# Experts' gather from fp32 token rows, and what is loaded in the places that this frees

## The reference

```python
# block 1
x = x + merged @ w_out                      # after attention and convolution branches
h2 = rms_norm(x, norm_ffn_g)                # 256 tokens x 1024
# router: top-1 of 4 groups, then top-2 of the 8 experts in that group
for g in range(N_GROUPS):                   # 4 groups x 8 experts, D_EXPERT = 256
    act = silu(h @ w_gate[g]) * (h @ w_up[g])
    act = act * combine[:, g]
    y = y + act @ w_down[g]
x = x + y
# block 2: attention and gated MLP mixer, layer norm, a dense SwiGLU (hidden 2816), layer norm
```

## Time and profile before

| | |
|---|---|
| runs | 699.73, 701.96, 703.51 us (median 701.96) |
| profiled execution | span 705.1 us; no other time of this execution is given |
| PE busy | 651.5 us, 92% |
| DVE / ACT / POOL busy | 336.3 us, 48% / 254.8 us, 36% / 18.2 us, 3% |
| moved by DMA | 186.06 MB, mean 264 GB/s |
| chain that ended last | PE 83%, DMA 8%, DVE 4%, issue 2% |

### The profile page before, as it was taken

How to read it: one execution, slowest core, us unless ns; L and a number is a source line. 1 busy time by engine, 2 the same in 40 slices (tenths; PEclk the granted TensorE clock), 3 DMA queues, 4 the chain that set the end, 5 groups by cost and what they waited for, 6 DMA issues and landing times.

```text
span 705.1 us, 11554 instructions
## 1 busy us (share of the span) xinstructions
PE 651.5 (92%) x4977; PEld 537.3 (76%) x4977; DVE 336.3 (48%) x417; ACT 254.8 (36%) x317; POOL 18.2 (3%) x11
## 2 busy tenths in 40 slices
PE   6999999999989988658877999999999999999995
PEld 5889999998856655335533577778889999999994
DVE  6754448756461121001110466776847444444447
ACT  6555453643411111000100455774146333333330
POOL 0000000000100000000000001420000000000000
PEclk9999999999999999976999999997999999999998
DMA  8969434787999999999999999153535555750001
GB/s 322 407 181 402 160 127 165 248 305 261 407 373 406 399 402 410 421 418 419 420 412 408 389 408 370 61 185 115 173 129 183 193 194 193 250 178 0 0 1 59
DMA packets 96219, 186.06 MB, mean 264 GB/s; under 512 B 9648, under 2 KB 33328, under 8 KB 96176
## 3 DMA queue, kind: packets, MB, share of 16 engines
q1 hardware_dynamic: 95888, 185.36, 70.8%
q10 hardware_dynamic: 288, 0.07, 0.0%
HBM read 184.37 MB, written 1.05 MB: 263 GB/s over the span
## 4 chain that ended last, share of the span: by engine, by line
PE 83%; DMA 8%; DVE 4%; issue 2%; SPq 1%; ACT 1%; DVEq 0%; ACTq 0%
PE ps L681 20%; PE ps L682 20%; PE ps L683 20%; DMA ring<-in_w_down_e 5%; PE ps L929 3%; PE ps L1003 3%; PE ps L958 3%; PE ps L1024 2%; PE ps L973 2%; PE ps L1036 2%; DMA ring<-in_w_up_e 2%; DMA X<-in_x 1%; PE ps L740 1%; SPq L508 1%; PE ps L813 1%
## 5 line engine op out<-in xcount | busy, mean ns | idle before, releaser
L1390 ACT ACTIVATE w_hi<-ring 128x2048 fp32r<-128x2048 f32 (+1 forms) x77 | 139.6, 1837 | 6.1 <-DMA ring<-in_w_in 5.6
L1844 DVE TENSOR_TENSOR w_lo<-ring,w_hi 128x2048 fp32r<-128x2048 f32 x47 | 107.4, 2296 | 34.2 <-ACT w_hi L1390 34.0
L681 PE MATMUL ps<-xT_hi,w_hi 128*128 128x256 f32 x320 | 90.6, 283 | 0.0
L683 PE MATMUL ps<-xT_hi,w_lo 128*128 128x256 f32 x320 | 90.6, 283 | 0.0
L682 PE MATMUL ps<-xT_lo,w_hi 128*128 128x256 f32 x320 | 90.5, 283 | 0.0
L681 PE MATMUL ps<-hR_hi,w_hi 128*128 128x256 f32 x224 | 64.0, 286 | 0.0
L682 PE MATMUL ps<-hR_lo,w_hi 128*128 128x256 f32 x224 | 63.4, 283 | 0.0
L683 PE MATMUL ps<-hR_hi,w_lo 128*128 128x256 f32 x224 | 63.3, 283 | 0.0
L682 PEld LDWEIGHTS ps<-xT_lo,w_hi 128*128 128x128 f32 x320 | 61.4, 192 | 0.4
L681 PEld LDWEIGHTS ps<-xT_hi,w_hi 128*128 128x128 f32 x320 | 61.4, 192 | 0.3
L683 PEld LDWEIGHTS ps<-xT_hi,w_lo 128*128 128x128 f32 x320 | 61.4, 192 | 0.0
(11 more groups left out here) (327 smaller groups left out, 1214.8 us busy)
## 6 DMA issues: line engine op xcount, KB each, us to landing
ring<-in_w_in SPq DMA_DIRECT2D x28, 1024.0 KB, 13.4
ring<-in_w_up_e SPq DMA_DIRECT2D x28, 1024.0 KB, 13.7
ring<-in_w_gate_e SPq DMA_DIRECT2D x27, 1024.0 KB, 11.8
ring<-in_w_down_e SPq DMA_DIRECT2D x26, 1024.0 KB, 16.7
ring<-in_w_gate SPq DMA_DIRECT2D x11, 1024.0 KB, 5.5
ring<-in_w_up SPq DMA_DIRECT2D x11, 1024.0 KB, 5.5
ring<-in_w_down SPq DMA_DIRECT2D x11, 1024.0 KB, 4.8
ring<-in_w_out SPq DMA_DIRECT2D x8, 1024.0 KB, 9.9
```

What stands on the lines that cost most here:

```text
L681: mm(o, a_hi, b_hi, start=start, stop=False, skip_group_check=True)
L683: return mm(o, a_lo, b_hi, start=False, stop=stop, skip_group_check=True)
L1390: return nc.scalar.activation(o, i, ACT.Copy)
L1844: tt(w_lo[slot][:], ring[:, slot, :], f32(upper_of(i)), ALU.subtract).then_inc(lo_made, 1)
```

## The change

`gather` reads `X` in fp32 with `pick` seen as fp32, and `xs_hi` and `xs_lo` are gone with their semaphores. `X` stays where it is until the experts are done. `early_c` moves to 176 KiB (over `ga`), a twelfth early unit `early_e` is put in four pieces of 2 KiB per partition (162, 200, 202 and 220 KiB), and both are loaded when `mgT_made` is 2. Four units are loaded again instead of three. `junk2`, a place for results that nobody reads, moves.

```diff
-EARLY = 11
-AGAIN = 3
+EARLY = 12
+AGAIN = 4
...
-        early_c = at("early_c", 168, [P, UNIT])
+        early_c = at("early_c", 176, [P, UNIT])
+        early_e = [at("early_e%d" % j, kib, [P, UNIT // QUAD]) for j, kib in enumerate((200, 202, 162, 220))]
...
-        junk2 = at("junk2", 220, [P, D], BF16)
+        junk2 = at("junk2", 192, [P, D], BF16)
...
         EARLY_AT = [(early_a, 0), (6, B1_PROJ), (7, B1_PROJ), (4, B1_UNITS - 4), (5, B1_UNITS - 4),
-                    (0, B1_UNITS - 3), (1, B1_UNITS - 2), (2, B1_UNITS - 1), (3, B1_UNITS), (early_b, 0), (early_c, 0)]
+                    (early_c, 0), (early_e, 0), (0, B1_UNITS - 3), (1, B1_UNITS - 2), (2, B1_UNITS - 1), (3, B1_UNITS),
+                    (early_b, 0)]
...
                     src = (wge if u < 4 else wue)[q, :, :, 2 * (u % 4):2 * (u % 4) + 2, :]
+                    if isinstance(dst, list):
+                        for j, part in enumerate(dst):
+                            sp.dma_start(part.rearrange("p (k f) -> p k f", k=2), src[:, j]).then_inc(landed, 16)
+                        return
...
-                elif spot is early_c:
-                    sp.wait_ge(xacc_ps, 1)
-                    sp.wait_ge(xslo_made, 1 + 2)
+                elif spot is early_c or spot is early_e:
+                    sp.wait_ge(mgT_made, 2)
...
                 if m == GU:
-                    early_unit(GU + 3)
-                    early_unit(GU + 4)
+                    for n in range(GU + 3, GU + 7):
+                        early_unit(n)
...
-                    early_unit(GU + 5 + m - GU)
+                    early_unit(GU + 7 + m - GU)
...
-            def gather(features, s, waits=False):
-
-                for part in range(2):
-                    for t in range(T):
-                        for k in features:
...
-                            last = mm(ps[:, 6 + k // 4, (k % 4) * P:(k % 4 + 1) * P], xs_lo(t, k) if part else xs_hi[:, t, k, :],
-                                      pick[:, t, :], start=(part == 0 and t == 0 and k % 4 == 0),
-                                      stop=(part == 1 and t == T - 1), skip_group_check=True)
+            def gather(features, s):
+
+                for t in range(T):
+                    for k in features:
+                        last = mm(ps[:, 6 + k // 4, (k % 4) * P:(k % 4 + 1) * P], X[:, t, k:D:KD],
+                                  pick[:, t, :].bitcast(F32), start=(t == 0 and k % 4 == 0), stop=(t == T - 1),
+                                  skip_group_check=True)
...
-                copy(xs_hi[:, t], X[:, t, :].rearrange("p (q k) -> p k q", k=KD)).then_inc(xshi_made, 1)
...
-            for dst, ks in ((xs_lo1a, slice(0, KD // 2)), (xs_lo1b, slice(KD // 2, KD))):
-                x = X[:, 1, :].rearrange("p (q k) -> p k q", k=KD)
-                tt(dst[:], x[:, ks, :], f32(xs_hi[:, 1, ks, :]), ALU.subtract).then_inc(xslo_made, 1)
...
-            xs_lower(0, ((xs_lo0, slice(0, KD)),))
```

More of the change, by code:

```diff
@@ L296, in build @@
         zy_ready = sem("zy_ready")
-        xshi_made = sem("xshi_made")
-        xslo_made = sem("xslo_made")
         h2a_made = sem("h2a_made")
@@ L301, in build @@
         wr_made = sem("wr_made")
-        xacc_ps = sem("xacc_ps")
         land_early_d = sem("land_early_d")
@@ L433, in early_area @@
             spot = EARLY_AT[early_spot(n)[0]][0]
+            if spot is early_e:
+                return [part[:] for part in early_e]
             return early[:, spot, :] if isinstance(spot, int) else spot[:]
@@ L546, in _ @@
                              ).then_inc(land_early_d, 16)
-            for n in range(GU + EARLY - 2, GU + EARLY):
-                early_unit(n)
+            early_unit(GU + EARLY - 1)
             for n in range(RING + EARLY + 1, 4 * UPQ):
@@ L911, in _ @@
             mm(ps[:, 7, 2 * NE:3 * NE], ones_b, asg[:, 1, :], start=False, stop=True).then_inc(rank_ps, 1)
[L912 to L918, removed]
-            def gather(features, s, waits=False):
-                for part in range(2):
-                    for t in range(T):
-                        for k in features:
[L925 to L928, removed]
-                            last = mm(ps[:, 6 + k // 4, (k % 4) * P:(k % 4 + 1) * P], xs_lo(t, k) if part else xs_hi[:, t, k, :],
-                                      pick[:, t, :], start=(part == 0 and t == 0 and k % 4 == 0),
-                                      stop=(part == 1 and t == T - 1), skip_group_check=True)
-                            if part and t == T - 1 and k % 4 == 3:
-                                last.then_inc(s["gath_ps"], 1)
+            x_in(0, 0)
+            def gather(features, s):
[4 more added lines that the diff above has]
+                                  skip_group_check=True)
+                        if t == T - 1 and k % 4 == 3:
+                            last.then_inc(s["gath_ps"], 1)
             def slot_weights(it, s):
@@ L980, in keep_busy, with quad_hidden @@
                     mm(ps[:, bank, 0:3 * P], ident_b, bfc[:].rearrange("p a n -> p (a n)"), start=True, stop=True)
-            def quad_hidden(it, s, weights, landed, waits=False, wide=False, fill=0):
+            def quad_hidden(it, s, weights, landed, wide=False, fill=0):
                 pe.wait_ge(s["pick_made"], it * 2 + 1)
                 pe.wait_ge(s["y_made"], it * 2 + 1)
-                gather(range(0, 6), s, waits)
+                gather(range(0, 6), s)
                 pe.wait_ge(s["turned_made"], it * 2 + 1)
@@ L996, in quad_hidden @@
                     wv = weights(u)
-                    if len(wv.shape) == 2:
-                        wv = wv.rearrange("p (a x) -> p a x", a=2)
-                    wv = wv.rearrange("p a (j k f) -> p a j k f", j=2, k=2)
+                    if isinstance(wv, list):
+                        rows = [part.rearrange("p (k f) -> p k f", k=2) for part in wv]
+                    else:
+                        if len(wv.shape) == 2:
+                            wv = wv.rearrange("p (a x) -> p a x", a=2)
+                        wv = wv.rearrange("p a (j k f) -> p a j k f", j=2, k=2)
+                        rows = [wv[:, j // 2, j % 2] for j in range(QUAD)]
                     for kk in range(2):
@@ L1003, in quad_hidden @@
                             last = mm(ps[32 * j:32 * j + 32, 4 + u // 4, 0:FE], heT[:, k, 32 * j:32 * j + 32],
-                                      wv[:, j // 2, j % 2, kk, :], start=(k == 0), stop=(k == KD - 1))
+                                      rows[j][:, kk, :], start=(k == 0), stop=(k == KD - 1))
                     last.then_inc(s["used"], 1)
@@ L1038, in quad_spread, with quad @@
                 last.then_inc(s["spread"], 1)
-            def quad(it, s, weights, landed, waits=False, wide=False):
-                quad_hidden(it, s, weights, landed, waits, wide)
+            def quad(it, s, weights, landed, wide=False):
+                quad_hidden(it, s, weights, landed, wide)
                 if wide:
@@ L1066, in wait @@
                         k, value = early_spot(n)
-                        pe.wait_ge(land_early[k], value)
+                        pe.wait_ge(land_early[k], value * (QUAD if EARLY_AT[k][0] is early_e else 1))
                     else:
@@ L1085, in _ @@
             for q in range(WIDE):
-                quad(q, first, weights_of(q), landed_of(q), q == 0)
+                quad(q, first, weights_of(q), landed_of(q))
             with pe.Fori(WIDE, OVER) as q:
@@ L2170, in _ @@
             slots(0, start0, 1)
-            dve.wait_ge(xshi_made, T)
-            dve.wait_ge(xslo_made, 1)
-            for dst, ks in ((xs_lo1a, slice(0, KD // 2)), (xs_lo1b, slice(KD // 2, KD))):
-                x = X[:, 1, :].rearrange("p (q k) -> p k q", k=KD)
-                tt(dst[:], x[:, ks, :], f32(xs_hi[:, 1, ks, :]), ALU.subtract).then_inc(xslo_made, 1)
             step(tt(emask, oh2, egrp, ALU.mult))
```

## The result

| | before | changed |
|---|---|---|
| median | 702.74 us (699.73 to 704.84, 4 runs) | 710.68 us (710.04 to 712.47, 4 runs) |
| ratio to before | 1 | 1.014, interval 1.0114 to 1.0167 |
| span of the profiled execution | 705.1 us | 708.5 us |

A forecast was written before the change was run, and what follows sets the result against it. Expert weight bytes through the load queue were taken as the bound. Gains of 1.5 us (hole), 0.2 us (second thin place) and 0.1 us rounding made -1.8 us: 701.96 to 700.2 us, range 697.4 to 702.8 us.

The forecast's parts named there:

- What bounds the kernel: Expert stage up to 381.7 us: arrival of weight bytes sets the end; PE, DVE and ACT have slack.
- the subtractions taken away: Vector work removed around the gather, with copies on ACT: covered by PE's gather, worth nothing.
- Gather: Per quad, 32 records stay 32 at 112 instead of 110 ns: 0.06 us, under the DMA wait, taken as nothing.
- The four passes: Gather on TensorE: by true fp32's four passes alone it would grow from 32 to 64; 128-column rows show no growth.
- The slower rival: Gather twice as long, +3.5 us a quad, queue dry before quad 1's first release: 5.8 us slower, 707.8 us; chance 0.06.
- Its threshold: The slower rival decides once the gather grows by over 2 us a quad.
- Loads, the hole: Queue at 196 to 208 us: two more MiB queued by 193.1 us fill it, gaining 1.5 us.
- the wait and the four small DMAs: SP blocked from 167.3 to 172.8 us, three more issues of some 0.4 us: queue stays alive, cost taken as nothing.
- early_d: First quad's late unit lands at 205.4 us, PE wants it at 205.0: PE stalls 0.4 us, bounds 0 and 1.5.
- Given back: Rival: hole is only uneven queue end, or thin place at 236 us opens equally; 1.5 us won and lost, 701.9 us; chance 0.20.
- The second thin place: Queue at 232 to 240 us, around quad 1's first release: just kept alive, margin 0.2 us; gain 0.2 us, bounds 0 and 0.6.

The follow-up runs named there:

- experiment 2: Kernel before with its two gather parts replaced by one contiguous fp32 copy of X, laid out chunk by chunk: 700.38 us, 0.9988.
- experiment 5: Contiguous fp32 gather of experiment 2 plus 36 extra gather records a quad: in quads 0 to 2 711.65 us, 1.0168; in quads 3 to 7 702.62 us, 1.0019.
- experiment 4: Gather weights 8 or 16 bytes apart in the fp32 copy of experiment 2: 701.4 and 713.71 us; 12 bytes apart in the changed kernel: 700.7 us.
- experiment 7: Changed kernel with the contiguous copy of experiment 2, early_c back on X and loaded last, early_e still at the merge: 698.59 us, 0.9966.
- experiment 6: Changed kernel with gather weights read from X 8 bytes apart instead of 32 (permuted, partly repeated features): 700.46 us, 1.0003.
- experiment 3: Kernel before with its fp32r parts laid out with the stride of X (32 bytes, 16 in the half parts): 734.33 us, one run.

## Why the prediction was wrong, point by point

- **What bounds the kernel**: right. Bytes set the end of the experts; the subtractions taken away brought nothing that can be told (experiment 2). But "PE, DVE and ACT have slack" holds for PE only from quad 3 on (experiment 5).
- **Gather**: the step that failed. "I take nothing, by the row of the same shape": the records measured 4.0 us more a quad, and in quads 0 to 2 no DMA wait covered them. The row chosen, L1198, has contiguous weights. The row with the stride, L740, was read by its spacing (111 ns), and transposes were taken for fp32 matmuls. Their own weight loads gave the warning. The group's rows of before for L740 (the strided `X`) and for L1148 (contiguous `qk`), both transposes, and the chain's row for eight of L1148:

```profile
L740 PEld LDWEIGHTS ps<-cst,X x48: 185/193/226, 4.7 to 512.8; 128*128 128x128 f32 x48
```

```profile
L1148 PEld LDWEIGHTS ps<-cst,qk x16: 138/140/143, 424.3 to 431.5; 128*128 128x128 f32 x16
```

```profile
424.68 0.87 PE ps L1148 x8
```

  193 against 140 ns: the stride costs 53 ns even there, and the spacing does not show it (111 ns, and 0.87/8 = 109 ns contiguous). A contiguous fp32 load of a matmul takes 192 ns at 112 ns a record; with 143 ns more there, the spacing becomes 233 ns. Why the same stride costs a transpose only 53 ns stays open.
- **The four passes** of the Trainium skill ("FP8 and Floating Point Precision", section TensorE Precision Notes) were weighed against the rows rightly: experiment 2 shows that they cost nothing at 128 columns. The rule of the Trainium skill that spoke against the change, the lines of 16 bytes (experiment 4), was missing from the sum.
- **The slower rival** was the right one in its mechanism and came too cheap: 5.8 us slower, for a PE that is 3.5 us late a quad; measured were 7.9 us, for 3.4. It named the right place, the release behind the thin place (238.8 forecast, 237.94 us measured), but it counted the lateness in quad 2 once and then called the rest covered; the windows show the queue thin again up to 288 us. Its chance, 0.06, was too small for a price whose only witness had another layout. Its threshold holds as far as it was tried: at 12 bytes the gather costs (4.12 + 1.60) - (2.63 + 1.04) = 2.05 us more a quad, and the one run took 700.7 us, with 341 GB/s at 232 to 240 us.
- **Loads, the hole**: it is filled, as forecast (405 GB/s at 204 to 208 us in experiment 7 and in the changed kernel). The size agrees with a contiguous gather (1.8 us forecast, some 1.8 between experiments 7 and 2), in part by luck, for there `early_c` is still loaded last and there is a dip of its own (338 GB/s at 172 to 176 us). In this change the size is not seen (experiment 6). Two small terms failed. "I take nothing" for the wait and the four small DMAs: 1.4 us in experiment 6. And `early_d`: 0.4 us forecast, 1.3 us measured there; it landed at 205.9 us for 205.4, and PE came for it at 204.6 us for 205.0. Issues were priced at 0.4 us each; with the fuller queue SP stood 2.4 us at many of them, and `early_b` was issued at 197.2 us and not at 193.1. Landings were close all the same: `early_b` at 208.7 us for 207.9, `early_c` at 179.8 for 178.6.
- **Given back**: its outcome, no gain, is what experiment 6 comes to, but not by its mechanism: there the second place does not open (412 GB/s at 232 to 240 us).
- **The second thin place** was seen. Its margin was worked out wrongly as 0.2 us, a fresh landing (236.7) against the queue's end (236.5); by the way that the prediction takes for `early_c` and for its rival, a fresh landing against the one behind the queue (239.1), it is 2.4 us. With PE 6.6 us late it became the loss: filling the first hole only lets the queue empty sooner while PE sets the pace.

## What to carry to other kernels

Price a strided operand by rows of the same operand role with the same stride, and look at the weight load's own duration, not at the spacing of a stream that may hide it. With fp32 weights keep at least two of them in each 16 bytes, or pay for one copy outside the loop: here two copies on ACT (2.2 and 2.0 us), for which PE does not stand, save 3.9 us of PE in each of eight quads. And in a stage bound by loads, PE's time is free only where PE waits for data; where loads wait for its releases, each lost microsecond counts.

## What the runs showed that was not expected

The fp32r gather with a stride (experiment 3) took 734 us, though its first and second gathers took 5.98 and 5.59 us as in fp32. The granted clock goes with it. Windows of it (for the changed kernel the row of 204 to 208 us stands in the first section, at 1.00):

```profile
200.00:204.00 4.00, 3.69 (x25) 2.47 (x24) 2.24 (x13) 0.00 (x0) 0.00 (x0) 0.69 0.63 242
204.00:208.00 4.00, 4.00 (x32) 2.82 (x32) 1.53 (x7) 0.00 (x0) 0.00 (x0) 0.50 0.52 192
```

Behind the slow fp32r gather the clock stood at 0.50, the lower of its levels (1.2 for 2.4 GHz), and the 16 matmuls after it took 1.94 us where the changed kernel takes 1.00. Behind the equally slow fp32 gathers of the first three quads it stayed at 1.00; it fell in the changed kernel too, but later (0.79 in the window of 272 to 280 us). Both gathers have 32 records a quad and the same weight loads, of 335 and 337 ns; they differ in type. What in that decides the clock was not tried and stays open, and experiment 3 is one run.
